# The tail of a one-core transformer block: transposes ahead of most folds, and half of the last norm shared by GpSimd and ScalarE

## The chip, the cores and the metric

The kernel runs as one program on one core of a Trainium2 chip. The time is the device time of one execution in microseconds (us). The kernel before was timed in three runs; the number quoted for it is their median. One further execution was recorded by the hardware profiler, and every duration below comes from that one. Its engines are TensorE (PE, with its weight loads PEld), VectorE (DVE), ScalarE (ACT), GpSimd (POOL) and the queue of SyncE (SP), which issues DMAs.

## The reference, cut to what matters

One layer: a modulated RMSNorm, an input projection into three kinds of heads, an output projection with a gated residual that gives `x1`, then a second modulated RMSNorm and a product-key expert layer (PEER), a second gated residual and a last RMSNorm. The change touches only the end:

```python
# peer: the expert layer's output for 256 tokens x 1024 channels
x = x + g2 * peer                                  # g2: one gate per channel
y = x * rsqrt(mean(x * x, axis=-1) + 1e-6)         # last RMSNorm
out = y * final_norm_g                             # one weight per channel
```

For each of 256 tokens the expert layer picks 16 experts of 16384 in each of 8 heads, and sums `gate * gelu(u_e . h) * v_e` over them.

## The kernel before, in words

All is float32. Tokens are numbered 0 to 255. The expert layer is computed in two ways at once. For the first ND = 160 tokens it is dense: TensorE streams the whole table `peer_u` through `u_chunk` (line 1034) and the whole table `peer_v` through `v_chunk` (line 1090), in 128 chunks each, and the products of gates and activations lie in `A3`. For the other 96 tokens GpSimd gathers the chosen rows by indirect DMAs (line 1917), and VectorE takes their dot products (line 1595) and adds them, weighted, into three tiles `sums[0..2]` (line 1608). Each of these tiles holds 32 tokens, a token's rows spread over four groups of 32 partitions.

The tail begins when the last chunk of `peer_v` has been multiplied. The dense result lies transposed, channels on partitions, in banks 4, 5 and 6 of PSUM, eight blocks `m` of 128 channels by 160 tokens. ScalarE copies banks 4 and 6 (lines 1380 and 1383) and VectorE bank 5 (line 1854) to the SBUF tile `OT`. TensorE then has three kinds of work, in this order:

- six folds (line 1113): a matmul with `fold4` sums the four partition groups of `sums[s]`, for a half (512 channels) of 32 tokens; banks 2 and 3, partitions 32 to 127;
- eight transposes (line 1123) of tokens 0 to 127 of `OT` into banks 0 and 1, four per half; `folded` is counted up once per half;
- eight matmuls (line 1127) that transpose tokens 128 to 159 into banks 2 and 3, partitions 0 to 31, four per half; `folded` again once per half.

So banks 0 to 3 hold the two halves of token block 0 (tokens 0 to 127) and of block 1 (tokens 128 to 255), numbered n = 0 to 3. VectorE runs, for each n, a multiplication of the bank by the gate `g2b` into a scratch place (line 1862; one input in PSUM, one in SBUF) and an addition of that to `x1n` (line 1863; both inputs in SBUF). ScalarE squares each sum with an accumulated row sum (line 1389). Per block VectorE adds the two row sums (`final_sum`, line 1867, two 128x1 inputs in SBUF), ScalarE takes the root (line 1392), VectorE the reciprocal (line 1872), and then VectorE multiplies both halves by the reciprocal and the weights `fin` (line 1874; two SBUF tensors and a per-partition pointer). The order of VectorE's work is written out: residuals 0, 1, 2, `final_sum(0)`, residual 3, `final_norm(0)`, `final_sum(1)`, `final_norm(1)`. SyncE's queue waits for each of the four half blocks in turn and issues its write to HBM (line 690). GpSimd has nothing to do in the tail; its last gather is issued some 30 us before the end of the span. `link` (line 1409) lets VectorE wait for its own instruction. Every engine works its instructions in the order written, and a wait holds up all that stand behind it on that engine. The weights `fin` are loaded into `gate_buf` once the gates are done (line 686).

Of the kernel before, what the change touches and what calls it, by code (L numbers as in the profile page):

```python
# [13 lines left out]
D = 1024  # L14
# [24 lines left out]
SUB = 32  # L39
# [192 lines left out]
LAST_TWO = (4 * SC2 + 2, 4 * SC2 + 3)  # L232

# [99 lines left out]
def build(nc, x_t, ctx_t, cols, rows, sgu_gain, final_gain, constants, sgu_wt, bias_mask, ada_w, w_in,  # L333
# [21 lines left out]
    with ExitStack() as stack:  # L355
# [172 lines left out]
        aside_full = sem("aside_full")  # L528
        own_full = [sem(f"own_full{n}") for n in range(len(OWN))]
# [89 lines left out]
        def _(sp):  # L619
# [67 lines left out]
            for n in range(2 * TB):  # L687
                tb, half = n // 2, slice(n % 2 * 512, n % 2 * 512 + 512)
                sp.wait_ge(out_ready, n + 1)
                sp.dma_start(out[tb * P:(tb + 1) * P, half], x1n[:, tb, half]).then_inc(stored, 16)  # L690
# [4 lines left out]
        def _(pe):  # L695
# [411 lines left out]
            pe.wait_ge(row_used, 2 * DOTS)  # L1107
            pe.wait_ge(a_made, CHUNKS)
            for half in range(2):
                hh = slice(half * 512, half * 512 + 512)  # L1110
                for s in range(SUBS):
                    rows = slice(ND1 + s * SUB, ND1 + (s + 1) * SUB)
                    pe.matmul(bank[2 + half][rows, :], fold4, sums[s][:, hh], start=True, stop=True,
                              tile_position=(0, ND1 + s * SUB))
            for half in range(2):
                for m in range(4 * half, 4 * half + 4):
                    if m == 0:
                        pe.wait_ge(act_out, 1)
                    elif m == 3:
                        pe.wait_ge(dve_out, 1)  # L1120
                    elif m == 6:
                        pe.wait_ge(act_out, 2)
                    mm = pe.transpose(bank[half][:, m % 4 * P:(m % 4 + 1) * P], OT[:, m, 0:P], ident)
                mm.then_inc(folded, 1)
            for half in range(2):
# [23 lines left out]
        def _(act):  # L1149
# [236 lines left out]
            for tb in range(TB):  # L1386
                for n in (2 * tb, 2 * tb + 1):
                    act.wait_ge(res_ready, n + 1)
                    act.activation(A[:, 12288 + n * 512:12288 + n * 512 + 512], x1n[:, tb, n % 2 * 512:n % 2 * 512 + 512], ACT.Square,
                                   accum_out=fsum[:, 0, n:n + 1]).then_inc(fsq_ready, 1)  # L1390
                act.wait_ge(fsum_ready, tb + 1)
                act.activation(fsum[:, 2, tb:tb + 1], fsum[:, 1, tb:tb + 1], ACT.Sqrt, bias=eps[:, :], scale=1.0 / D)\
                   .then_inc(froot_ready, 1)

# [11 lines left out]
        def _(dve):  # L1406
# [450 lines left out]
            def residual(n):  # L1857

                tb, half = n // 2, slice(n % 2 * 512, n % 2 * 512 + 512)
                tmp = A[:, 10240 + n * 512:10240 + n * 512 + 512]  # L1860
                dve.wait_ge(folded, n + 1)
                link(dve.tensor_tensor(tmp, bank[n][:, :], g2b[:, half], ALU.mult))
                dve.tensor_tensor(x1n[:, tb, half], x1n[:, tb, half], tmp, ALU.add).then_inc(res_ready, 1)
# [6 lines left out]
            def final_norm(tb):  # L1870
                dve.wait_ge(froot_ready, tb + 1)
                link(dve.reciprocal(fsum[:, 1, TB + tb:TB + tb + 1], fsum[:, 2, tb:tb + 1]))
                for half in (slice(0, 512), slice(512, D)):
                    dve.scalar_tensor_tensor(x1n[:, tb, half], x1n[:, tb, half], fsum[:, 1, TB + tb:TB + tb + 1],
                                             fin[:, half], ALU.mult, ALU.mult).then_inc(out_ready, 1)

            residual(0)
            residual(1)
            residual(2)
            final_sum(0)  # L1880
            residual(3)
            dve.wait_ge(fin_in, 16)
            dve.wait_ge(res_ready, 2 * TB)
# [6 lines left out]
        def _(pool):  # L1890
# [55 lines left out]
            for n in range(DOTS, 2 * DOTS):  # L1946
                gather(n)

# [75 lines left out]
```

## Time and profile before

| | us |
|---|---|
| median of 3 runs | 890.07 |
| lowest, highest run | 887.4, 891.44 |
| the profiled execution's own time | 888.64 |
| its span in the profile | 886.9 |
| PE busy in the span | 857.2 (97%) |
| DVE busy | 542.9 (61%) |
| ACT busy | 281.1 (32%) |
| POOL busy | 271.2 (31%) |

The span runs from the first to the last recorded event of the execution; its own time is 1.74 us longer, since it also holds what lies around the span. A busy share is an average over stages that have different limits, so for a change to the tail only the rows of the tail tell what it is worth. In the timeline each row gives a start, a duration, engine, line, operation, output <- inputs with their shapes, and in brackets the engine's idle time before it and what ended that. Rows of matmuls merge many instructions; their ends are modelled. The chain of waits is followed back from the last instruction: at each step to what released it.

### The profile page before, as it was taken

How to read it: one execution, taken by the hardware profiler on the slowest of the kernel's cores; microseconds unless marked ns; L12 is line 12 of the kernel's file. 1: busy time of each engine (PE TensorE's matmuls, PEld its weight loads, DVE VectorE, ACT ScalarE, POOL GpSimd, SP SyncE). 2: the span in 40 equal slices, each digit the busy share in tenths (PEclk: the TensorE clock that was granted, in tenths of full speed). 3: DMA queues.
4: the chain of work that ended last, by engine and by line, in shares of the span. 5: the costliest groups of instructions: out<-in, count | busy, mean ns of one | idle time of the engine just before them, and what ended most of it. 6: DMA issues, size and time to landing. Idle time of an engine off the chain costs nothing.

```text
span 886.9 us, 17756 instructions
## 1 busy us (share of the span) xinstructions
PE 857.2 (97%) x6620; PEld 815.3 (92%) x6620; DVE 542.9 (61%) x1073; ACT 281.1 (32%) x684; POOL 271.2 (31%) x245
## 2 busy tenths in 40 slices
PE   3999999999999999999999999999999999999995
PEld 1889996797979999999999999999999999999994
DVE  4567146675899789874547888886333444334447
ACT  4364336856332111122137888860000000000002
POOL 0020002402342343335346433546222223222220
PEclk9999999999999999999999999999999999999998
DMA  9987465042495899999999999999999999999992
GB/s 370 399 325 270 174 231 214 1 191 95 143 331 160 321 409 410 409 399 395 409 409 409 409 396 331 306 356 394 409 409 409 409 409 408 409 409 409 409 409 110
DMA packets 74558, 294.28 MB, mean 332 GB/s; under 512 B 9218, under 2 KB 9346, under 8 KB 67972
## 3 DMA queue, kind: packets, MB, share of 16 engines
q1 hardware_dynamic: 37444, 161.24, 47.0%
q0 software_dynamic: 28416, 100.78, 29.6%
q10 hardware_dynamic: 8640, 31.46, 8.9%
q8 instruction: 40, 0.66, 0.3%
q14 instruction: 18, 0.15, 0.0%
HBM read 290.73 MB, written 1.05 MB: 329 GB/s over the span
## 4 chain that ended last, share of the span: by engine, by line
PE 89%; DMA 4%; DVE 3%; ACT 3%; issue 1%; SPq 0%; ACTq 0%; DVEq 0%; POOL 0%
PE bank L1090 31%; PE bank L1034 29%; PE bank L713 5%; PE bank L714 4%; PE bank L715 4%; PE bank L1043 4%; PE bank L733 2%; DMA stage<-in_peer_u_t 2%; DMA A<-in_ada_w 2%; PE bank L976 1%; PE bank L813 1%; PE bank L752 1%; PE bank L822 1%; PE bank L958 1%; ACT A L1256 1%
## 5 line engine op out<-in xcount | busy, mean ns | idle before, releaser
L1034 PE MATMUL bank<-A,stage 128*128 128x160 f32 x2048 | 286.2, 299 | 0.5 <-DMA stage<-in_peer_u_t 0.2
L1034 PEld LDWEIGHTS bank<-A,stage 128*128 128x128 f32 x2048 | 279.6, 190 | 1.5 <-issue 1.1
L1090 PE MATMUL bank<-A,stage 128*128 128x160 f32 x2048 | 278.3, 299 | 0.0
L1090 PEld LDWEIGHTS bank<-A,stage 128*128 128x128 f32 x2048 | 278.2, 190 | 0.0
L1608 DVE SCALAR_TENSOR_TENSOR sum<-A,row_gate,sum 128x1024 f32<-128x1024 f32 x81 | 104.0, 1284 | 132.8 <-DMA A<-in_peer_v,row_expert 131.5
L1917 POOL DMA_INDIRECT A<-in_peer_v,row_expert x84 | 83.7, 996 | 165.2 <-DVE sum L1608 147.9
L1595 DVE CUSTOM_DVE_ANT_0 A<-A 128x1024 f32<-128x1024 f32 x80 | 97.7, 1222 | 51.7 <-DMA A<-in_peer_u,row_expert 51.5
L1917 POOL DMA_INDIRECT A<-in_peer_u,row_expert x80 | 91.3, 1141 | 122.0 <-DVE row_dot L1595 66.0
L1380 ACT ACTIVATE A<-bank 128x480 f32<-128x480 f32 x1 | 0.6, 572 | 276.3 <-PE bank L1090 276.3
L1312 ACT ACTIVATE A<-bank 128x160 f32 (+1 forms) x88 | 26.7, 303 | 150.3 <-PE bank L1034 150.3
L715 PE MATMUL bank<-h_hi,ring_low 128*128 128x256 f32 x224 | 63.3, 283 | 0.0
L1334 ACT ACTIVATE gate_buf<-gate_buf,choice_t 128x128 f32<-128x128 f32 x160 | 51.1, 390 | 4.4
L1327 ACT ACTIVATE gate_buf<-con,choice_t 128x128 f32<-128x128 f32 x160 | 50.7, 390 | 0.6 <-issue 0.6
L1043 PE MATMUL bank<-gate_buf 128*128 128x128 f32 x320 | 43.7, 280 | 0.9 <-ACT gate_buf L1334 0.9
L1043 PEld LDWEIGHTS bank<-gate_buf 128*128 128x128 f32 x320 | 38.9, 191 | 4.7 <-issue 4.4
L715 PEld LDWEIGHTS bank<-h_hi,ring_low 128*128 128x128 f32 x224 | 42.9, 191 | 0.0
L1401 POOL TENSOR_TENSOR ring_low<-A,lo 128x512 fp32r<-128x512 f32 x4 | 5.0, 1270 | 91.3 <-ACT lo L1218 91.3
L733 PE MATMUL bank<-A,csil 128*32 128x256 f32 x208 | 16.1, 441 | 13.5 <-DMA A<-in_ada_w 13.5
L1917 POOL DMA_INDIRECT last_row<-in_peer_u,row_expert x16 | 20.1, 1259 | 28.8 <-DVE row_dot L1595 20.6
L1810 DVE TENSOR_TENSOR gate_buf<-con,choice_t 128x512 f32<-128x512 f32 x40 | 27.3, 685 | 0.0
L1818 DVE TENSOR_TENSOR A<-A,bank 128x512 f32<-128x512 f32 x40 | 27.1, 679 | 0.0
L1824 DVE TENSOR_TENSOR A<-A,choice 128x160 f32<-128x160 f32 x40 | 13.0, 325 | 22.8 <-ACT choice L1319 22.8
(271 smaller groups left out, 1221.7 us busy)
## 6 DMA issues: line engine op xcount, KB each, us to landing
stage<-in_peer_u_t SPq DMA_DIRECT2D x128, 512.0 KB, 10.0
stage<-in_peer_v SPq DMA_DIRECT2D x68, 512.0 KB, 7.8
stage<-in_peer_v ACTq DMA_DIRECT2D x60, 512.0 KB, 8.4
A<-in_ada_w SPq DMA_DIRECT2D x13, 1024.0 KB, 7.4
A<-in_w_in SPq DMA_DIRECT2D x11, 1024.0 KB, 6.7
stage<-in_ada_w SPq DMA_DIRECT2D x10, 1024.0 KB, 6.9
A<-in_w_q SPq DMA_DIRECT2D x8, 1024.0 KB, 7.4
A<-in_w_out SPq DMA_DIRECT2D x4, 1024.0 KB, 4.8
```

What stands on the lines that cost most here:

```text
L713: pe.matmul(o, a_hi, b_hi, start=(k == 0), stop=False)
L714: pe.matmul(o, a_hi, b_lo, start=False, stop=False)
L715: mm = pe.matmul(o, a_lo, b_hi, start=False, stop=(k == KD - 1))
L733: mm = pe.matmul(o[q, 0:BLK], csil[:, k, :], w[:, k, :], start=(k < 4), stop=(k >= 4), tile_position=(0, 32 * (k % 4)))
L1034: mm = pe.matmul(o, stage[j][:, k * P:(k + 1) * P], H2[:, k, 0:ND], start=(k == 0), stop=(k == KD - 1))
L1043: mm = pe.matmul(bank[4 + j][:, t * NK:(t + 1) * NK], ONE1[:, j, t, :], ONE2[:, j, t, :], start=True, stop=True)
L1090: mm = pe.matmul(bank[b][:, n * ND:(n + 1) * ND], stage[c % SLOTS][:, m * P:(m + 1) * P], A3[:, c, :], start=(c == 0 and n == 0), stop=(c ...
L1327: last = act.activation(ONE2[:, j % 2, t, :], iota, ACT.Square, bias=choice_t[:, 0, bass.ds(g * GT + t, 1)])
L1334: last = act.activation(ONE2[:, j % 2, t, :], ONE2[:, j % 2, t, :], ACT.Relu, bias=choice_t[:, 2, bass.ds(g * GT + t, 1)], scale=-2.0)
L1595: dve.tensor_tensor_reduce(g, g, h2_rows[:, s, :], 1.0, 0.0, ALU.mult, ALU.add, row_dot[:, s, c:c + 1])\
L1608: dve.scalar_tensor_tensor(sums[s][:, :], g, w, sums[s][:, :], ALU.mult, ALU.add)\
L1917: pool.indirect_dma_start(gathered[slot], None, peer_u if n < DOTS else peer_v, bass.IndirectOffsetOnAxis(ap=row_expert[:, s, c:c + 1], ax ...
```

## The change

It has three parts.

1. On TensorE, two folds (the first two tiles, first half) come first, then the eight transposes, then the other four folds (the third tile's first half, all three of the second half), then the matmuls of tokens 128 to 159. The wait for all rows of `sums` moves behind the transposes; ahead of them stands a wait for the rows of the first two tiles alone.
2. The addition of n = 1 goes from VectorE to GpSimd. The multiplications and additions on VectorE are written apart and wait for each other by the semaphore `res_scaled`; VectorE's order is now: scale 0, add 0, scale 1, scale 2, add 2, scale 3, `final_sum(0)`, add 3, `final_norm(0)`, `final_sum(1)`, `final_norm(1)`.
3. Of the last norm, VectorE keeps the first half of each block. For the second half GpSimd multiplies `x1n` by the weights `fin` into a scratch place as soon as that half is summed (`gained`), and ScalarE multiplies this by VectorE's reciprocal (`root_turned`), as a Copy whose scale is a per-partition pointer. ScalarE's order is: squares 0, 1, 2, root of block 0, square 3, second half of block 0, root of block 1, second half of block 1. SyncE's queue waits for the two halves by two semaphores, in the same order of writes as before.

```diff
--- before.py
+++ after.py
@@ -232,6 +232,9 @@
 LAST_TWO = (4 * SC2 + 2, 4 * SC2 + 3)
 
 
+POOL_ADDS = 1
+
+
 def row_slot(n):
 
     return n % GATHER if n < EARLY else (n - EARLY) % WIDE_GATHER
@@ -526,6 +529,8 @@
             sem, ("consts_in", "x_in", "ctx_in", "cols_in", "gating_in", "bias_in", "subkeys_in", "g2_row_in"))
         own_split = sem("own_split")
         aside_full = sem("aside_full")
+        res_scaled, res_added, gained, root_turned, act_out_ready = map(
+            sem, ("res_scaled", "res_added", "gained", "root_turned", "act_out_ready"))
         own_full = [sem(f"own_full{n}") for n in range(len(OWN))]
         ring_full = [[sem(f"ring{r}_full{s}") for s in range((RING, RING, SIDE)[r])] for r in range(3)]
         bank_full = [sem(f"bank_full{b}") for b in range(8)]
@@ -686,7 +691,10 @@
             sp.dma_start(fin, final_gain).then_inc(fin_in, 16)
             for n in range(2 * TB):
                 tb, half = n // 2, slice(n % 2 * 512, n % 2 * 512 + 512)
-                sp.wait_ge(out_ready, n + 1)
+                if n % 2:
+                    sp.wait_ge(act_out_ready, n // 2 + 1)
+                else:
+                    sp.wait_ge(out_ready, n // 2 + 1)
                 sp.dma_start(out[tb * P:(tb + 1) * P, half], x1n[:, tb, half]).then_inc(stored, 16)
             sp.wait_ge(stored, 16 * 2 * TB)
 
@@ -1104,14 +1112,16 @@
                 v_chunk(c)
 
 
-            pe.wait_ge(row_used, 2 * DOTS)
+            def fold(s, half):
+
+                rows, hh = slice(ND1 + s * SUB, ND1 + (s + 1) * SUB), slice(half * 512, half * 512 + 512)
+                pe.matmul(bank[2 + half][rows, :], fold4, sums[s][:, hh], start=True, stop=True,
+                          tile_position=(0, ND1 + s * SUB))
+
             pe.wait_ge(a_made, CHUNKS)
-            for half in range(2):
-                hh = slice(half * 512, half * 512 + 512)
-                for s in range(SUBS):
-                    rows = slice(ND1 + s * SUB, ND1 + (s + 1) * SUB)
-                    pe.matmul(bank[2 + half][rows, :], fold4, sums[s][:, hh], start=True, stop=True,
-                              tile_position=(0, ND1 + s * SUB))
+            pe.wait_ge(row_used, 2 * DOTS - ROWS)
+            for s in range(SUBS - 1):
+                fold(s, 0)
             for half in range(2):
                 for m in range(4 * half, 4 * half + 4):
                     if m == 0:
@@ -1122,6 +1132,10 @@
                         pe.wait_ge(act_out, 2)
                     mm = pe.transpose(bank[half][:, m % 4 * P:(m % 4 + 1) * P], OT[:, m, 0:P], ident)
                 mm.then_inc(folded, 1)
+            pe.wait_ge(row_used, 2 * DOTS)
+            fold(SUBS - 1, 0)
+            for s in range(SUBS):
+                fold(s, 1)
             for half in range(2):
                 for m in range(4 * half, 4 * half + 4):
                     mm = pe.matmul(bank[2 + half][0:ND1, m % 4 * P:(m % 4 + 1) * P], OT[:, m, P:ND], ident,
@@ -1383,14 +1397,38 @@
             act.activation(OT[:, 6:8, :].rearrange("p m t -> p (m t)"), bank[6][:, 0:2 * ND], ACT.Copy)\
                .then_inc(act_out, 1)
             act.activation(fsum[:, 2, TB:TB + 1], eps[:, :], ACT.Sqrt)
-            for tb in range(TB):
-                for n in (2 * tb, 2 * tb + 1):
-                    act.wait_ge(res_ready, n + 1)
-                    act.activation(A[:, 12288 + n * 512:12288 + n * 512 + 512], x1n[:, tb, n % 2 * 512:n % 2 * 512 + 512], ACT.Square,
-                                   accum_out=fsum[:, 0, n:n + 1]).then_inc(fsq_ready, 1)
+            def squared(n):
+
+                if n == POOL_ADDS:
+                    act.wait_ge(res_added, 1)
+                else:
+                    act.wait_ge(res_ready, n + 1 - (n > POOL_ADDS))
+                tb, half = n // 2, slice(n % 2 * 512, n % 2 * 512 + 512)
+                act.activation(A[:, 12288 + n * 512:12288 + n * 512 + 512], x1n[:, tb, half], ACT.Square,
+                               accum_out=fsum[:, 0, n:n + 1]).then_inc(fsq_ready, 1)
+
+            def final_root(tb):
+
                 act.wait_ge(fsum_ready, tb + 1)
                 act.activation(fsum[:, 2, tb:tb + 1], fsum[:, 1, tb:tb + 1], ACT.Sqrt, bias=eps[:, :], scale=1.0 / D)\
                    .then_inc(froot_ready, 1)
+
+            def scaled_out(tb):
+
+                act.wait_ge(gained, tb + 1)
+                act.wait_ge(root_turned, tb + 1)
+                at = 10240 + (2 * tb + 1) * 512
+                act.activation(x1n[:, tb, 512:D], A[:, at:at + 512], ACT.Copy,
+                               scale=fsum[:, 1, TB + tb:TB + tb + 1]).then_inc(act_out_ready, 1)
+
+            squared(0)
+            squared(1)
+            squared(2)
+            final_root(0)
+            squared(3)
+            scaled_out(0)
+            final_root(1)
+            scaled_out(1)
 
 
         def quarter_rest(eng, n):
@@ -1854,13 +1892,20 @@
             dve.tensor_copy(OT[:, 3:6, :].rearrange("p m t -> p (m t)"), bank[5][:, 0:3 * ND]).then_inc(dve_out, 1)
 
 
-            def residual(n):
+            def scaled_at(n):
+                return A[:, 10240 + n * 512:10240 + n * 512 + 512]
+
+            def scale_residual(n):
+
+                half = slice(n % 2 * 512, n % 2 * 512 + 512)
+                dve.wait_ge(folded, n + 1)
+                dve.tensor_tensor(scaled_at(n), bank[n][:, :], g2b[:, half], ALU.mult).then_inc(res_scaled, 1)
+
+            def add_residual(n):
 
                 tb, half = n // 2, slice(n % 2 * 512, n % 2 * 512 + 512)
-                tmp = A[:, 10240 + n * 512:10240 + n * 512 + 512]
-                dve.wait_ge(folded, n + 1)
-                link(dve.tensor_tensor(tmp, bank[n][:, :], g2b[:, half], ALU.mult))
-                dve.tensor_tensor(x1n[:, tb, half], x1n[:, tb, half], tmp, ALU.add).then_inc(res_ready, 1)
+                dve.wait_ge(res_scaled, n + 1)
+                dve.tensor_tensor(x1n[:, tb, half], x1n[:, tb, half], scaled_at(n), ALU.add).then_inc(res_ready, 1)
 
             def final_sum(tb):
                 dve.wait_ge(fsq_ready, 2 * tb + 2)
@@ -1869,18 +1914,20 @@
 
             def final_norm(tb):
                 dve.wait_ge(froot_ready, tb + 1)
-                link(dve.reciprocal(fsum[:, 1, TB + tb:TB + tb + 1], fsum[:, 2, tb:tb + 1]))
-                for half in (slice(0, 512), slice(512, D)):
-                    dve.scalar_tensor_tensor(x1n[:, tb, half], x1n[:, tb, half], fsum[:, 1, TB + tb:TB + tb + 1],
-                                             fin[:, half], ALU.mult, ALU.mult).then_inc(out_ready, 1)
-
-            residual(0)
-            residual(1)
-            residual(2)
+                dve.reciprocal(fsum[:, 1, TB + tb:TB + tb + 1], fsum[:, 2, tb:tb + 1]).then_inc(root_turned, 1)
+                dve.wait_ge(root_turned, tb + 1)
+                dve.scalar_tensor_tensor(x1n[:, tb, 0:512], x1n[:, tb, 0:512], fsum[:, 1, TB + tb:TB + tb + 1],
+                                         fin[:, 0:512], ALU.mult, ALU.mult).then_inc(out_ready, 1)
+
+            scale_residual(0)
+            add_residual(0)
+            scale_residual(POOL_ADDS)
+            scale_residual(2)
+            add_residual(2)
+            scale_residual(3)
             final_sum(0)
-            residual(3)
+            add_residual(3)
             dve.wait_ge(fin_in, 16)
-            dve.wait_ge(res_ready, 2 * TB)
             final_norm(0)
             final_sum(1)
             final_norm(1)
@@ -1945,6 +1992,18 @@
                         .then_inc(gate_in, 16)
             for n in range(DOTS, 2 * DOTS):
                 gather(n)
+            pool.wait_ge(res_scaled, POOL_ADDS + 1)
+            tb, half = POOL_ADDS // 2, slice(POOL_ADDS % 2 * 512, POOL_ADDS % 2 * 512 + 512)
+            at = 10240 + POOL_ADDS * 512
+            pool.tensor_tensor(x1n[:, tb, half], x1n[:, tb, half], A[:, at:at + 512], ALU.add).then_inc(res_added, 1)
+            pool.wait_ge(fin_in, 16)
+            for tb in range(TB):
+                if tb == 0:
+                    pool.wait_ge(res_added, 1)
+                else:
+                    pool.wait_ge(res_ready, 2 * TB - 1)
+                at = 10240 + (2 * tb + 1) * 512
+                pool.tensor_tensor(A[:, at:at + 512], x1n[:, tb, 512:D], fin[:, 512:D], ALU.mult).then_inc(gained, 1)
 
 
 def bias_places():
```

## Rows read from the trace of the kernel before

**Rows 1.** The page, part 4: the chain that ended last, by engine

```profile
PE 89%; DMA 4%; DVE 3%; ACT 3%; issue 1%; SPq 0%; ACTq 0%; DVEq 0%; POOL 0%
```

**Rows 2.** The chain, from 860 us on: start, us, what

```profile
874.53 0.60 PE bank L1123 x4
882.43 0.30 ACT fsum L1392
882.96 0.75 DVE x1n L1874
```

**Rows 3.** Timeline, 872 to 876 us: start, us, engine, line, operation

```profile
872.45 0.65 DVE L1854 COPY A<-bank 128x480 f32<-128x480 f32 x1
872.62 1.92 PE L1113 MATMUL bank<-sum,con 128*32 128x512 f32 x12
872.72 0.44 ACT L1383 ACTIVATE A<-bank 128x320 f32<-128x320 f32 x1 [0.79 <-PE bank L1090]
874.47 1.09 PE L1123 MATMUL bank<-con,A 128*128 128x128 f32 x8
875.16 0.69 DVE L1862 TENSOR_TENSOR A<-bank,g2b 128x512 f32<-128x512 f32 x1 [2.06 <-PE bank L1123]
875.49 1.94 PE L1127 MATMUL bank<-con,A 128*32 128x128 f32 x16
```

**Rows 4.** Timeline, 877 to 881 us, DVE and ACT, same columns

```profile
877.82 0.68 DVE L1862 TENSOR_TENSOR A<-bank,g2b 128x512 f32<-128x512 f32 x1
878.54 0.69 DVE L1863 TENSOR_TENSOR x1n<-x1n,A 128x512 f32<-128x512 f32 x1
879.15 0.15 DVE L1867 TENSOR_TENSOR fsum<-fsum 128x1 f32<-128x1 f32 x1
879.53 0.61 ACT L1389 ACTIVATE A<-x1n 128x512 f32<-128x512 f32 x1
880.05 0.19 ACT L1389 ACTIVATION_READ_ACCUMULATOR A<-x1n 128x1 f32 x1
```

**Rows 5.** GpSimd: line 1401 (ns min/median/max), then two from the timeline

```profile
L1401 POOL TENSOR_TENSOR ring_low<-A,out_hi x8: 1261/1276/1297, 157.0 to 170.9; 128x512 fp32r<-128x512 f32 x8
195.97 0.63 ACT L1271 ACTIVATE A<-A 128x512 f32<-128x512 f32 x1
196.68 0.74 POOL L1902 TENSOR_TENSOR A<-A 128x256 f32<-128x256 f32 x1 [24.53 <-ACT A L1271]
```

**Rows 6.** Timelines of GpSimd and of VectorE; last, line 1507 (ns)

```profile
50.99 3.77 POOL L1896 TENSOR_TENSOR A<-A 128x1024 f32<-128x1024 f32 x2 [50.54 <-ACT A L1226]
50.99 6.52 POOL L1896 TENSOR_TENSOR A<-A 128x1024 f32<-128x1024 f32 x3 [50.54 <-ACT A L1226]
53.52 3.40 DVE L1507 TENSOR_TENSOR ring_low<-A,lo 128x2048 fp32r<-128x2048 f32 x1 [2.73 <-ACT lo L1204]
252.07 4.80 POOL L1906 TENSOR_TENSOR ring_low<-A,query_hi 128x2048 fp32r<-128x2048 f32 x1 [7.38 <-ACT query_hi L1204]
253.78 3.14 DVE L1584 SCALAR_TENSOR_TENSOR A<-choice 128x32 uint32<-128x32 f32 x1
L1507 DVE TENSOR_TENSOR ring_low<-A,query_hi x3: 2284/2285/2293, 192.4 to 213.9; 128x2048 fp32r<-128x2048 f32 x3
```

**Rows 7.** ScalarE lines 1281 and 1223 (ns); a root in the timeline

```profile
L1281 ACT ACTIVATE A<-A,mod x8: 492/493/508, 205.5 to 210.2; 128x256 f32<-128x256 f32 x8
L1223 ACT ACTIVATE h_hi<-A x8: 399/410/419, 151.7 to 190.1; 128x256 fp32r<-128x256 f32 x8
178.25 0.69 ACT L1145 ACTIVATE gate_buf<-bank,eps 128x512 f32<-128x512 f32 x1
```

**Rows 8.** Last two writes' issues; stretches, last columns DMA share and GB/s

```profile
883.73 0.99 SPq L690 DMA_DIRECT2D out_x<-x1n  x2
884.40:884.60 0.20, 0.00 (x0) 0.00 (x0) 0.00 (x0) 0.00 (x0) 0.00 (x0) 0.50 0.19 72
885.80:886.00 0.20, 0.00 (x0) 0.00 (x0) 0.00 (x0) 0.00 (x0) 0.00 (x0) 0.50 0.75 277
```

## Prediction

> **What bounds the kernel now.** The page's chain by engine comes first: TensorE carries 89% of it, VectorE and ScalarE 3% each, and GpSimd nothing [rows 1]. The reader sees from it that a change behind TensorE's last chunk can only touch a few per mille. The body, up to 872.6 us of a span of 886.9, is left as it is by the diff; what is priced here is the 14.3 us behind it. The chain of that stretch [rows 2] and its timeline [rows 3, 4] show three steps. TensorE runs six folds, then transposes; only when four transposes are done, at 875.16, can VectorE start (it had been free since 873.10). From there VectorE alternates multiplication and addition without a pause and sets the pace. At the end comes a short relay for block 1, root, reciprocal, product: the root starts at 882.43, the product at 882.96, and its first half ends at 883.71 [rows 2].
>
> **What sets the end.** The last two writes are issued from 883.73, the second as soon as its half is ready, 0.66 us later (0.99 us for two issues of 0.33) [rows 8]. DMA traffic starts within 884.40 to 884.60 (share 0.19, so at about 884.56) and ends within 885.80 to 886.00 (share 0.75, so at about 885.95): 1.4 us for two writes of 256 KB, 0.7 each, back to back [rows 8]. The first write's issue therefore sets the end. If the second half comes earlier its write only queues behind the first. So I measure everything by one moment: the end of VectorE's product for the first half of block 1, now 883.71. That ScalarE finishes the other half at the same time, not 0.7 us later, is worth nothing.
>
> **TensorE.** Six folds took from 872.62 to 874.47, 0.31 each; the eight transposes 1.02; the first product on VectorE started 0.69 after the first transpose [rows 3]. With two folds ahead the transposes start at 872.62 + 0.62 = 873.24, and scale 0 at 873.93, not 875.16. The copies that the transposes wait for, at 873.10 (VectorE) and 873.16 (ScalarE) [rows 3], are just in time, the first being asked for by the fourth transpose at about 873.6. But the work ahead of the last eight matmuls is the same six folds and eight transposes, so they start at 875.49 as before and take 1.94 [rows 3]: bank 2 is full at about 876.50, bank 3 at 877.43. Of the 1.23 us won for n = 0 and 1, what is late next is bank 2.
>
> **VectorE up to there.** Multiplication to addition is 0.72 from start to start, addition to the next 0.61 [rows 4]. Scale 0 873.93, add 0 874.65, scale 1 875.26 to 875.94. Scale 2 waits 0.6 us for bank 2, 876.50 in place of 877.82 [rows 4]; add 2 is ready at 877.22. Taking add 1 away saves VectorE 0.6 us, but that falls into this wait. So far we are 1.32 us ahead.
>
> **GpSimd's three instructions.** Its TENSOR_TENSOR of 128x512 took 1.28 (1.26 to 1.30), and it starts 0.08 after what it waited for (196.60 to 196.68) [rows 5]. The addition for n = 1 runs 876.02 to 877.30. The question is what GpSimd costs VectorE. Two places show it. At 53.52 VectorE's line 1507, two SBUF inputs, met GpSimd: GpSimd's second addition ended at 54.76, VectorE at 56.92, after 3.40 in place of 2.29, and GpSimd's third ended at 57.51 [rows 6]. VectorE's end is 2.16 after GpSimd's, its own duration less 0.13; GpSimd's third, 0.74 when alone [rows 5], ended 0.59 after VectorE. At 253.78 an instruction over only 32 columns took 3.14, until 256.92, just as GpSimd's 4.80 ended at 256.87 [rows 6]. I read: VectorE instructions with two SBUF inputs and GpSimd's TENSOR_TENSOR exclude each other, and the one that waited ends 0.13 to 0.15 short of a full duration after the other. The multiplications read a bank and one SBUF tile; I take them as free. The additions, both final sums and the products with `fin` have two SBUF inputs.
> The Trainium skill, "SBUF — State Buffer", in the section on who interferes with whom, states an exclusive lock for the whole instruction. The trace agrees with the exclusion but shows the head start of 0.13 to 0.15; taking the rule to its letter, with full durations behind each release, the moment would come at 883.52 and the time be 889.9.
>
> **The sum.** Add 2, waiting since 877.22, ends at 877.91. GpSimd's product for block 0 is ready at 877.35, waits for add 2, and ends at 877.91 + 1.13 = 879.04. A square takes 0.71 from start to the end of its accumulator [rows 4]: square 1 from 877.35 to 878.06, square 2 to 878.77. `final_sum(0)`, a 128x1 addition of 0.15 [rows 4], could run at 878.44 but has two SBUF inputs: it waits for GpSimd and ends at 879.09. Behind it on VectorE stands add 3: 879.01 to 879.70. Root 0 ends at 879.42, hidden. From root to product are 0.23 us for the reciprocal and its waits (882.73 to 882.96) [rows 2]; here the product 0 is ready at 879.85, GpSimd's product for block 1 at 879.78, and either may win. If GpSimd does, it ends at 881.06, VectorE at 881.68, `final_sum(1)` at 881.75; if VectorE does, GpSimd ends at 881.73 and `final_sum(1)` at 881.78. The two agree. Square 3 is done at 880.45 and hidden. Root 1 0.33 later, product from 882.34, first half finished at 883.09. **The gain is 883.71 - 883.09 = 0.6 us.**
>
> **ScalarE.** Its scaled Copy of 128x512 I price at 0.61 [rows 4] plus 0.08 for the pointer, the difference of 493 and 410 ns between lines 1281 and 1223 [rows 7]: 0.7. The first runs 880.45 to 881.15, ahead of root 1, which can't start before 881.78: hidden by GpSimd's hold on VectorE; without that cover it is on the path (rival 1). The second runs beside VectorE's last product, and its write queues behind. Copies of line 1223 follow the root of 178.25 [rows 7] with no table load among ScalarE's rows until the Gelus, so I expect none here. If one were needed for each change between Copy and Sqrt, two loads would stand ahead of root 1.
> SyncE's split waits, VectorE's extra semaphore waits and TensorE's moved wait cost nothing: the same waits were there as `link`, and all gathered rows are summed before VectorE's copy of 872.45 [rows 3], which stands behind them.
>
> **Rivals.**
> 1. *No exclusion worth the name*: GpSimd's instructions interfere little. `final_sum(0)` ends at 878.59, add 3 at 879.20, product 0 starts at 879.33; square 3 ends at 879.95, then the Copy of 0.7 stands ahead of root 1, which ends at 880.96; product 1 ends at 881.94. Gain 1.8, time 888.3. Against it stand both places of [rows 6]; for it only that neither has TensorE and ScalarE in this tail. Chance 0.15.
> 2. *GpSimd keeps its turn* (slower): its product for block 0 goes ahead of add 2. Then add 2 ends at 877.35 + 1.28 + 0.56 = 879.19, add 3 at 880.48, GpSimd's product 1 at 881.84, VectorE's product 0 at 882.46, `final_sum(1)` at 882.53, and the moment is 883.84: 0.13 later than before, time 890.2. It decides as soon as add 2 is ready over 0.13 us later than 877.22, that is if bank 2 fills after 876.63. For it: my 876.50 is a modelled end. Against: in [rows 6] VectorE, waiting first, went ahead of GpSimd's next. Chance 0.3.
> The Trainium skill, "SBUF — State Buffer", the same section, has a rule for this one: issue order decides who blocks. GpSimd's product needs nothing but its own addition; if it counts as issued behind it at once, the rule gives rival 2, and no row here separates the two.
> 3. *The parts cancel otherwise*: TensorE's order brings less than shown, since the copies come late by more than 0.5 us, and the time stays at 890.1. Both copies end at least 0.4 us ahead of their need. Chance 0.05.
> The forecast has 0.5.
>
> **How the numbers follow.** The profiled execution's own time is 888.64, 1.43 below the median of 890.07; its forecast is 888.0, and that of the median 890.07 - 0.6 = 889.5. The three runs lie between 887.4 and 891.44, which is more than any case here moves. The range takes in rival 1 at 888.3 and rival 2 at 890.2 and about 1 us of that scatter on each side: 887.3 to 891.2. A measurement of this kernel tells about 0.5%, 4.5 us, from no change: faster would need under 885.6, slower over 894.5. The largest gain is 1.8, the largest loss 0.13, so only scatter or something unseen in the body leads there: 0.04 and 0.03, and 0.93 for within.
>
> **What would show it.** In the profile after, counted from the end of line 1090's last matmul: VectorE's first multiplication 1.2 us after it, not 2.5; an idle VectorE before scale 2, ended by TensorE; `final_sum(0)` of line 1867 lasting over 0.5 us, not 0.15; the first or second GpSimd product longer than 1.28; no table load behind the last root; two output issues back to back, with 1.4 us of traffic. A `final_sum` of 0.15 everywhere means rival 1. An addition for n = 2 of over 1.5 us means rival 2. The forecast is wrong if the moment comes over 1 us from 0.6 us ahead of before, or if the stretch ahead of the tail differs.

## The result, and the profile after

The changed kernel takes 892.92 us (median of 20 runs, 889.82 to 894.29); the kernel before takes 889.07 in 20 runs (887.25 to 892.56). The ratio is 1.0031, with a 95% interval of 1.0021 to 1.0041: slower by 2.8 us. The means, 892.34 and 889.53, lie 2.8 us apart, the medians 3.85. The profiled execution's own time is 891.03 and its span 888.9, 2.0 more than before.

The timeline of the changed kernel's tail answers to [rows 3] and [rows 4]; columns are start, us, engine, line, operation, and idle time before with its releaser.

```profile
872.03 1.05 PE L1118 MATMUL bank<-sum,con 128*32 128x512 f32 x4
872.13 0.44 ACT L1397 ACTIVATE A<-bank 128x320 f32<-128x320 f32 x1 [0.79 <-PE bank L1098]
...
873.01 1.09 PE L1133 MATMUL bank<-con,A 128*128 128x128 f32 x8
873.70 0.69 DVE L1902 TENSOR_TENSOR A<-bank,g2b 128x512 f32<-128x512 f32 x1 [1.21 <-PE bank L1133]
...
875.81 1.26 POOL L1998 TENSOR_TENSOR x1n<-x1n,A 128x512 f32<-128x512 f32 x1 [19.04 <-DVE A L1902]
876.04 0.69 DVE L1902 TENSOR_TENSOR A<-bank,g2b 128x512 f32<-128x512 f32 x1 [0.32 <-PE bank L1141]
876.77 0.85 DVE L1908 TENSOR_TENSOR x1n<-x1n,A 128x512 f32<-128x512 f32 x1
...
877.21 1.54 POOL L2006 TENSOR_TENSOR A<-x1n,gate_buf 128x512 f32<-128x512 f32 x1
...
878.14 0.62 DVE L1912 TENSOR_TENSOR fsum<-fsum 128x1 f32<-128x1 f32 x1
...
878.69 0.68 DVE L1908 TENSOR_TENSOR x1n<-x1n,A 128x512 f32<-128x512 f32 x1
...
879.45 1.27 POOL L2006 TENSOR_TENSOR A<-x1n,gate_buf 128x512 f32<-128x512 f32 x1 [0.70 <-DVE x1n L1908]
879.47 1.79 DVE L1919 SCALAR_TENSOR_TENSOR x1n<-x1n,fsum,gate_buf 128x512 f32<-128x512 f32 x1
...
880.03 0.71 ACT L1421 ACTIVATE x1n<-A,fsum 128x512 f32<-128x512 f32 x1
...
881.36 0.29 ACT L1413 ACTIVATE fsum<-fsum,eps 128x1 f32<-128x1 f32 x1 [0.63 <-DVE fsum L1912]
...
881.89 0.75 DVE L1919 SCALAR_TENSOR_TENSOR x1n<-x1n,fsum,gate_buf 128x512 f32<-128x512 f32 x1
881.95 0.72 ACT L1421 ACTIVATE x1n<-A,fsum 128x512 f32<-128x512 f32 x1 [0.29 <-DVE fsum L1917]
```

To compare profiles I count from the start of ScalarE's copy of bank 6, which begins as the last matmul of the chunks ends: 872.72 before [rows 3], 872.13 here. VectorE and ScalarE are ahead of the kernel before all the way. VectorE's first multiplication starts at +1.57 (before +2.44), and the moment of the forecast, the end of VectorE's product for the first half of block 1, comes at +10.51 (before +10.99). GpSimd's and VectorE's two-input instructions shut each other out, as the trace of the kernel before had let one expect: `final_sum(0)` of 128x1 lasts 0.62 us, VectorE's product of block 0 1.79, GpSimd's product 1.54. ScalarE is done at 882.67. Yet the span ends at 888.9, 6.2 us later. SyncE's queue had issued its last write by 883.50 (the last three issues in one row):

```profile
881.68 1.82 SPq L698 DMA_DIRECT2D out_x<-x1n  x3
```

The instructions at the end of the program, which count as no engine's busy time, show the rest. In this view (one source line; duration in ns min/median/max, first and last start in us) the changed kernel has:

```profile
L358 POOLq DRAIN  x1: 9235/9235/9235, 879.4 to 879.4; - x1
...
L358 SPq DRAIN  x1: 7/7/7, 885.6 to 885.6; - x1
L358 SPq EVENT_SEMAPHORE  x1: 17/17/17, 888.8 to 888.8; - x1
```

The same view of the kernel before:

```profile
L355 POOLq DRAIN  x1: 18257/18257/18257, 856.3 to 856.3; - x1
...
L355 SPq DRAIN  x1: 7/7/7, 886.6 to 886.6; - x1
L355 SPq EVENT_SEMAPHORE  x1: 17/17/17, 886.8 to 886.8; - x1
```

Each engine closes with a DRAIN, an instruction that stands behind all its others; SyncE's comes behind its wait for the last write. In all 13 profiles of this document the span ends 0.2 us behind the later of two of them, SyncE's and GpSimd's. The row of a DRAIN can start while the instruction ahead of it still runs, so what counts is its end. Before, GpSimd's drain stood behind its last gather (856.48 to 857.42) and was over at 874.5, hidden by the whole tail; the end followed SyncE's drain of 886.6 by 0.2 us. Now GpSimd works until 880.71, and its drain ends at 888.64: 7.93 us behind its last instruction, and 3.1 us after SyncE's drain of 885.6. The tail, from the start of ScalarE's copy to the end of the span, is 16.74 us and was 14.13: 2.61 longer, where SyncE's drain alone would have made it 0.49 shorter.

The span doesn't hold all of the time. What lies around it (own time less span, mean over all timed runs, each span known to 0.1 us) is 1.79 to 1.80 us in the kernel before and 2.15 in the changed one. This 0.35 us comes on top of the 2.61; why it is there was not tried.

### The profile page after: what moved, and what is told of

Same layout as the page of the kernel before. It is cut to its first block, busy times and chain, and to the rows that moved or that the text cites. A ratio compares the mean times of both kernels' runs of the same rounds, so it can differ in the third digit from the quotient of the medians.

```text
span 888.9 us, 17761 instructions
## 1 busy us (share of the span) xinstructions
PE 854.4 (96%) x6620; PEld 812.9 (91%) x6620; DVE 542.4 (61%) x1070; ACT 282.6 (32%) x686; POOL 276.8 (31%) x248
## 4 chain that ended last, share of the span: by engine, by line
PE 85%; DMA 6%; ACT 3%; DVE 2%; issue 1%; POOL 1%; SPq 0%; ACTq 0%; DVEq 0%
PE bank L1098 31%; PE bank L1042 27%; PE bank L721 4%; PE bank L1051 4%; PE bank L722 4%; PE bank L723 4%; DMA stage<-in_peer_u_t 4%; PE bank L741 2%; DMA A<-in_ada_w 2%; PE bank L760 1%; PE bank L821 1%; PE bank L830 1%; PE bank L984 1%; PE bank L966 1%; DMA A<-in_w_q 1%
## 5 line engine op out<-in xcount | busy, mean ns | idle before, releaser
L1964 POOL DMA_INDIRECT A<-in_peer_u,row_expert x80 | 94.3, 1178 | 119.9 <-DVE row_dot L1633 76.6
```

What stands on the lines that cost most here:

```text
L1964: pool.indirect_dma_start(gathered[slot], None, peer_u if n < DOTS else peer_v, bass.IndirectOffsetOnAxis(ap=row_expert[:, s, c:c + 1], ax ...
```

## The experiments

Theory D: GpSimd's closing drain, some 8 us behind its last instruction whatever that is, ends the program. Rival P: the products on GpSimd cost VectorE the time. Rival T: the drain is long only behind a TENSOR_TENSOR. Rival G: the drain ends the program, but it is long only because of the gathers, and a drain taken earlier makes it short. The table gives every profile in us, counted from the start of ScalarE's copy of bank 6 (last GpSimd instruction's end, closing drain's end, SyncE's drain, end of the span), and the measured ratio to the kernel before, timed beside it, with its 95% interval. Where a kernel has a second drain, the third column is that of the closing one. order_sum_ahead and best are each measured twice.

| kernel | last GpSimd | its drain | SyncE's drain | end | ratio (interval) |
|---|---|---|---|---|---|
| before | -15.31 | 1.79 | 13.91 | 14.13 | 1 |
| changed | 8.58 | 16.51 | 13.42 | 16.74 | 1.0031 (1.0021 to 1.0041) |
| late_memset | 8.29 | 16.23 | 14.12 | 16.46 | 1.0026 (1.0012 to 1.0040) |
| no_last_product | 6.63 | 14.56 | 12.70 | 14.79 | 1.0009 (0.9993 to 1.0025) |
| add_alone | 4.93 | 12.87 | 12.89 | 13.11 | 0.9983 (0.9970 to 0.9997) |
| mid_drain | 15.10 | 23.01 | 19.94 | 23.25 | one run, 898.66 us |
| after_early_drain | 9.27 | 9.34 | 14.12 | 14.34 | 0.9993 (0.9980 to 1.0005) |
| after_early_drain_2 | 8.58 | 8.65 | 13.42 | 13.64 | 1.0000 (0.9985 to 1.0014) |
| order_alone | -15.35 | 1.80 | 13.04 | 13.26 | 0.9994 (0.9981 to 1.0008) |
| order_sum_ahead | -14.06 | 2.26 | 12.60 | 12.82 | 0.9982 (0.9971 to 0.9993) |
| order_sum_ahead_2 | -13.27 | 2.59 | 12.65 | 12.87 | 0.9986 (0.9974 to 0.9999) |
| best | 4.93 | 5.00 | 12.46 | 12.68 | 0.9993 (0.9982 to 1.0005) |
| best_2 | 4.93 | 5.01 | 12.46 | 12.68 | 0.9987 (0.9972 to 1.0001) |

**One idle instruction on GpSimd, late.**

```diff
--- kernel before
+            pool.wait_ge(res_ready, 2 * TB)
+            pool.memset(spare[:, :], 0.0).then_inc(late, 1)
```

The tile `spare` (128x1) and the semaphore `late` are declared besides.

> The kernel before, plus one GpSimd memset of 128x1 into a tile nobody reads, waiting for the last residual. Tail = span end less the start of ScalarE's copy of bank 6: 14.2 us before, 16.8 in the changed kernel. Theory D (GpSimd's closing drain takes about 8 us after its last instruction, whatever that is, and the program ends behind it): the memset runs about 8.0 us into the tail, the drain ends 8 us later, tail 16.3 to 16.5, time +2.2 us. Rival P (the changed kernel lost its time to products on GpSimd that hold up VectorE): tail 14.2, no change. Rival T (the drain is long only behind a TENSOR_TENSOR): tail 14.2, drain under 2 us behind the memset.

GpSimd's timeline and the closing instructions of this kernel:

```profile
881.57 0.10 POOL L1951 MEMSET spare<- 128x1 f32 x1 [22.79 <-DVE x1n L1865]
```

```profile
L355 POOLq DRAIN  x1: 8050/8050/8050, 881.5 to 881.5; - x1
...
L355 SPq DRAIN  x1: 7/7/7, 887.5 to 887.5; - x1
L355 SPq EVENT_SEMAPHORE  x1: 17/17/17, 889.8 to 889.8; - x1
```

A memset of 0.10 us, whose result nobody reads, ends at 881.67; the drain ends at 881.5 + 8.05, 7.94 behind it by the table, 2.1 after SyncE's. The time rises by 0.26%, the end in the table by 2.33 us, which is 0.26% of 889. No part of the change is in this kernel. Rival T falls, and rival P isn't needed for the loss. Theory D and rival G both fit so far.

**The same change with GpSimd's drain taken earlier.**

```diff
--- changed kernel
             for n in range(DOTS, 2 * DOTS):
                 gather(n)
+            pool.drain()
             pool.wait_ge(res_scaled, POOL_ADDS + 1)
```

> The changed kernel with one drain more on GpSimd, behind its last gather and ahead of its first work in the tail, where GpSimd idles for 19 us. Theory D (about 8 us fixed behind any last instruction): the closing drain stays at about 8 us and the tail at 16.8. Rival G (the closing drain is long since it settles the gathers' descriptors, once): the early drain takes that over, unseen, the closing one ends by the time of SyncE's last wait, tail 13.7 to 13.9, 3 us faster than the changed kernel.

> The changed kernel with the drain on GpSimd ahead of the tail, once more, since in the first profile VectorE's rows came 1.4 us late. With rows on time (VectorE's copy of bank 5 within 0.3 us of ScalarE's of bank 6) the tail should be 13.6 to 13.7; then sharing the halves costs 0.5 to 0.6 us against the addition alone (13.1), by GpSimd's products holding up final_sum(0) and VectorE's product of block 0. Time -0.5 against before.

The second run's GpSimd row, the added drain (line 1995), and the closing instructions:

```profile
881.98 1.27 POOL L2007 TENSOR_TENSOR A<-x1n,gate_buf 128x512 f32<-128x512 f32 x1 [0.70 <-DVE x1n L1908]
```

```profile
L1995 POOLq DRAIN  x1: 17201/17201/17201, 859.8 to 859.8; - x1
```

```profile
L358 POOLq DRAIN  x1: 1375/1375/1375, 881.9 to 881.9; - x1
...
L358 SPq DRAIN  x1: 7/7/7, 888.1 to 888.1; - x1
L358 SPq EVENT_SEMAPHORE  x1: 17/17/17, 888.2 to 888.2; - x1
```

The added drain takes 17.20 us from 859.8 to 877.0, while GpSimd waits anyway for VectorE's first results. The closing drain now starts with the product of 881.98 and lasts 1.38: it ends 0.07 us behind that product. The end of the span is SyncE's again. The tail is 13.64, 3.1 shorter than in the changed kernel, with every other instruction of the change in its place; the ratios 0.9993 and 1.0000 have intervals that don't touch that of the changed kernel. So the drain is the loss. Theory D in its first form (8 us behind any last instruction, tail 16.8) missed here, and rival G forecast it. That it is the gathers since the last drain, and not GpSimd's other work or the time since then, is the likely reading but not shown: no kernel here has a long stretch without gathers behind a drain. Against the kernel before this tail is 0.49 us shorter, but the measured time doesn't show it: both intervals hold 1, and what lies around the span is 2.04 to 2.06 us, 0.25 more than there. In the first of the two runs VectorE's copy of bank 5 came at +1.19, with the rows late, and that execution's tail is 0.70 longer.

**Half the gathers behind the last drain.**

```diff
--- changed kernel
+            pool.drain()
             for n in range(DOTS, 2 * DOTS):
                 gather(n)
```

> The changed kernel with a drain on GpSimd half way, between the 96 gathers of the first table (with the loads of row_gate) and the 96 of the second, and none ahead of the tail. The closing drain now stands behind half of GpSimd's DMAs. If its length is their number (so much per DMA not yet settled), it ends about 4.0 to 4.5 us behind GpSimd's last product, tail 13.7 to 13.9. If it is a fixed price for any gather since the last drain, it stays at 7.9, tail 16.7. The body may be longer, since the drain holds the second gathers up; only the tail is read.

```profile
887.23 1.27 POOL L2007 TENSOR_TENSOR A<-x1n,gate_buf 128x512 f32<-128x512 f32 x1 [2.51 <-DVE x1n L1908]
```

```profile
L358 POOLq DRAIN  x1: 9219/9219/9219, 887.2 to 887.2; - x1
```

GpSimd's last product ends at 888.50 and the drain at 887.2 + 9.22 = 896.4, 7.91 behind. Half the gathers, the same price: it isn't so much per gather. The forecast tail of 16.7 was missed, for another reason. The added drain lasted until 585.5, 9.9 us behind the last DMA that GpSimd had issued (of line 1990), so the second table's first gather was issued at 586.28, against 574.70 in the changed kernel. The rows came late, VectorE's copy of bank 5 started at +5.32, and the tail is 23.25. Only the closing drain's length is read from this kernel. What GpSimd does in those 7.9 us these profiles don't show.

**GpSimd's work cut step by step.** First without its last product:

```diff
--- changed kernel
+SHARED = (0,)
...
-            for tb in range(TB):
+            for tb in SHARED:
                 ...
                 pool.tensor_tensor(A[:, at:at + 512], x1n[:, tb, 512:D], fin[:, 512:D], ALU.mult).then_inc(gained, 1)
```

VectorE makes both halves of block 1, and ScalarE only the second half of block 0. The waits of VectorE, ScalarE and SyncE follow; VectorE waits for all four sums ahead of its first product.

> The changed kernel, but VectorE makes both halves of block 1's last product; GpSimd ends with its product for block 0. Drain theory: GpSimd's last instruction ends 6.5 to 6.7 us into the tail, its drain 7.95 later at 14.5, tail 14.7 to 14.8, that is +0.6 against the kernel before and -2.0 against the changed one. If the drain weren't what ends the program, the tail would be VectorE's, 13.3 to 13.6.

```profile
878.63 1.53 POOL L2014 TENSOR_TENSOR A<-x1n,gate_buf 128x512 f32<-128x512 f32 x1
```

```profile
L359 POOLq DRAIN  x1: 9495/9495/9495, 878.6 to 878.6; - x1
```

The drain ends 7.93 behind the product of 880.16, 1.9 after SyncE's. Then without both products; the addition for n = 1 is all that GpSimd keeps:

```diff
--- changed kernel
+SHARED = ()
...
-            for tb in range(TB):
+            for tb in SHARED:
```

> The changed kernel without its third part: GpSimd makes only the addition for n = 1 and VectorE both halves of both blocks' last product. Theory D: GpSimd's last instruction ends about 5.0 us into the tail, its drain at 13.0, hidden behind the writes; the tail is VectorE's, 12.9 to 13.3, time -1.0 to -1.3 against before. Rival P (only contention matters): the same tail here, so this run tells D from P only together with the memset. Theory X (any GpSimd work in the tail costs some 3 us at the end): tail 15 or more.

The addition ends at +4.93 and the drain at +12.87, a hair ahead of SyncE's at +12.89: just hidden. Theory X of the expectation (15 us or more with any GpSimd work in the tail) falls: the end is +13.11, 1.02 less than before, and the ratio of 0.9983 (to 0.9997) is faster than before. The same GpSimd is on the path or off it by when its last instruction ends. Four kernels with an undrained queue of gathers (8.58, 8.29, 6.63 and 4.93) give 7.93, 7.94, 7.93 and 7.94.

**Part 1 alone.** The kernel before with TensorE's new order and nothing else:

```diff
--- kernel before
-            pe.wait_ge(row_used, 2 * DOTS)
             pe.wait_ge(a_made, CHUNKS)
-            for half in range(2):
-                ...
+            pe.wait_ge(row_used, 2 * DOTS - ROWS)
+            for s in range(SUBS - 1):
+                fold(s, 0)
             for half in range(2):
                 ...
+            pe.wait_ge(row_used, 2 * DOTS)
+            fold(SUBS - 1, 0)
+            for s in range(SUBS):
+                fold(s, 1)
```

`fold` is the function of the changed kernel.

> The kernel before with part 1 alone: TensorE's transposes ahead of four folds. No GpSimd in the tail. All theories: VectorE starts 1.2 us earlier and, taking 1.33 us for each multiplication and addition, reaches scale 2 at about the moment bank 2 fills, so it keeps all of it: tail 13.0 in place of 14.2, time -1.2 us. If bank 2 bounds instead, scale 2 waits and the tail is 13.1 to 13.5.

The end comes 0.87 earlier, not 1.2: VectorE starts at +1.57, not +2.44, and keeps all of it, since scale 2 starts at +4.23 without a wait. The tail of 13.26 lies in the range that the expectation gives for a wait for bank 2, but there was none: the smaller start explains it. The ratio, 0.9994 (0.9981 to 1.0008), can't tell 0.87 us (0.9990) from none; the profile can.

**Two versions meant to beat both kernels.** To part 1 alone:

```diff
--- order_alone
-                for half in (slice(0, 512), slice(512, D)):
+                for h in range(2):
+                    half = slice(h * 512, h * 512 + 512)
                     ...
+                    if tb == 0 and h == 0:
+                        final_sum(1)
             final_norm(0)
-            final_sum(1)
             final_norm(1)
```

> The kernel with part 1 alone, and final_sum(1) put between VectorE's two products of block 0, so that ScalarE's root for block 1 runs beside the second. No GpSimd in the tail. VectorE's first product of block 1 starts 0.4 us earlier: tail 12.8 to 12.9 in place of 13.26, time -1.3 against before. If the first write of block 1 is held up behind the second of block 0 on the DMA queues, the tail stays within 0.2 of 13.26.

> The same kernel as order_sum_ahead, once more beside best: tail 12.8, time -1.3 us against before (ratio 0.9985), within 0.2 us of best.

And with GpSimd's addition and the early drain besides:

```diff
--- add_alone
                 gather(n)
+            pool.drain()
             pool.wait_ge(res_scaled, POOL_ADDS + 1)
...
+                if tb == 0:
+                    final_sum(1)
                 if tb not in SHARED:
                     ...
             final_norm(0)
-            final_sum(1)
             final_norm(1)
```

> Part 1, GpSimd's addition for n = 1 (no product on GpSimd or ScalarE), a drain on GpSimd behind its last gather, and final_sum(1) between the two products of block 0. Drain theory: the closing drain is over 1.4 us after GpSimd's start of that addition's drain, far ahead of SyncE's; tail 12.6 to 12.7, time -1.4 against before. Against order_sum_ahead the addition on GpSimd is worth 0.1 to 0.2, since VectorE waits for bank 2. If the early drain delays the last gathers' rows, VectorE's copy of bank 5 comes over 1 us late and nothing is gained.

> The same kernel as best, once more beside order_sum_ahead: tail 12.7, time -1.4 us against before (ratio 0.9984). If the early drain costs something in the body, the tail is 12.7 again but the ratio is nearer to 1 than that of order_sum_ahead_2.

`order_sum_ahead` ends at +12.82 and +12.87 and is faster than the kernel before in both measurements, 0.9982 and 0.9986, with both intervals below 1. Its first write of block 1 wasn't held up, which would have left the tail within 0.2 of 13.26. The version with the addition on GpSimd ends 0.14 to 0.19 earlier in its profiles, as expected, but measures 0.9993 and 0.9987 with intervals that reach 1. The intervals of the two overlap, so a difference in the measured time isn't shown. But what lies around the span can account for the missing lead: it is 1.96 to 1.97 us in `best` and 1.80 to 1.81 in `order_sum_ahead` (1.79 in `add_alone`, which has GpSimd's addition but no early drain). The version to take is `order_sum_ahead`, which puts no new work on GpSimd or ScalarE.

## Why the prediction was wrong

I forecast 889.5 from 890.07, 0.6 us faster, with a range of 887.3 to 891.2. Measured are 892.92 and, by the ratio, 2.8 us slower. Point by point:

- **What sets the end: the step that failed.** "The first write's issue therefore sets the end. ... So I measure everything by one moment." This moment came 0.48 us earlier than before, and the time rose. The end has two conditions, SyncE's wait for its writes and the other engines' closing drains, of which GpSimd's is the late one. The first is as I had it: SyncE's drain ended 2.92 us behind the moment before and 2.91 after. In the trace of before the second was met 12.1 us ahead of SyncE's (1.79 against 13.91) and appears in neither the chain nor the busy times. What GpSimd does behind its last instruction was put at nothing, and what hid it was not named: GpSimd had finished early, and the change took that away. "GpSimd, nothing" in the chain said only that its drain was hidden. With the step mended by the measured 7.93 behind the last product, which I had at 881.06 on the scale of before, the drain ends at 888.99 and the span at 889.2 in place of 886.9, 2.3 us slower. Measured are 2.61 in the tail, since the last product ended 8.58 us into it and not 8.34, and 0.35 more around the span.
- **TensorE's order.** Right in kind, too large in size. I spread 1.85 us evenly over six folds, 0.31 each. But the folds of a half use three different groups of columns and run at once (the rows of the last section): three folds take the time of one, and so do two. Two folds took 0.98 (872.03 to 873.01), six 1.85. VectorE's start was 0.87 us earlier, not 1.23. Most of this error of 0.36 us fell into VectorE's wait for bank 2, which was 0.32 long and not 0.6: scale 2 started 3.91 us into the tail, 0.13 later than the forecast of 3.78.
- **GpSimd's three instructions.** The addition took 1.26 (forecast 1.28), and the first product, waiting, ended 1.13 after add 2 (877.62 to 878.75), as priced. Add 2 itself ended 0.55 after GpSimd's addition, not beside it: 0.85 long in place of 0.69, 0.16 us that I had taken for none. `final_sum(0)` ended 0.01 after GpSimd's product. Of the race for block 1, GpSimd won (879.45 against 879.47), and VectorE's product ended at 881.26, 0.54 after GpSimd's end. That the other order would cost the same no run shows.
- **The rule on the pair of SBUF ports** (the Trainium skill, "SBUF — State Buffer", section "Who interferes with whom"). It states an exclusive lock for the whole instruction. These rows show the exclusion once more, but not full durations behind each release: VectorE's product of 0.75 ended 0.54 after GpSimd's, GpSimd's of 1.27 ended 1.13 after add 2. Rival 2's reading of issue order did not come about: add 2, which had been waiting, went ahead of GpSimd's queued product in the changed kernel and in both after_early_drain profiles.
- **ScalarE.** Its scaled Copy took 0.71 (forecast 0.70), with no table load behind it.
- **The sum of the tail without the drain.** after_early_drain_2 has the changed kernel's tail with the drain out of the way, row by row on VectorE: 13.64 against 14.13, 0.49 us shorter; the forecast was 0.6. So apart from the drain the sum came out to 0.1 us, in part by luck: the error of 0.36 in TensorE's order fell into a wait.
- **The rivals.** None contained the mechanism, and the largest loss that I allowed for was 0.13 us. The slower rival, GpSimd going ahead of add 2, was worth just that, a twentieth of the loss. No `final_sum(0)` of 0.15 (it lasted 0.62) and no add 2 of over 1.5 us (0.85): by their own signs rivals 1 and 2 both fell. Rival 3 fell with VectorE's earlier start.

## What to carry to other kernels

When work is put on an engine that had finished early, look at what that engine still has to do behind its last instruction: in this kernel GpSimd's closing drain needed 7.9 us after gathers, so its last instruction had to end 8 us ahead of SyncE's drain, or the drain had to be taken beforehand, where the engine waits anyway. The chain and the busy times leave such instructions out; the view of the line that holds the closing instructions (355 before, 358 after) shows them. And sharing work between VectorE and GpSimd lengthened VectorE's instructions with two SBUF inputs that met GpSimd's (0.15 to 0.62 us, 0.75 to 1.79). A plain reordering of the same work on VectorE (0.87 us by TensorE's order, 0.4 more by one moved `final_sum`) was worth more than three engines sharing it.

## What the runs showed of the hardware that was not expected

- GpSimd's closing drain ended 7.91 to 7.94 us behind its last instruction in five kernels, whatever that was (a memset of 0.10 us or a product of 1.27) and though its last gather had been issued over 18 us before that. After 96 gathers it was the same as after 192. With a drain between gathers and last instruction it ended 0.07 us behind it. A drain right behind the last gather took longer, 14.9 to 17.2 us from that gather's end in eight profiles. In all eight it ended 4.4 us behind the last packet of GpSimd's DMA queue (4.38 to 4.43; in the kernel before the last packet ended at 870.12 and the drain at 874.51), so most of it is the wait for the gathered data. The 4.4 us don't hold for every drain: that of mid_drain at line 1993, behind the loads of `row_gate`, ended 8.9 us behind the queue's last packet.
- Matmuls of 32 columns in different groups of TensorE's array run at once. In the kernel before the six folds (two passes each) come in four groups of three matmuls, at 872.62, 873.07, 873.50 and 873.93, though each matmul lasts 0.59 or more. Their weight loads run up to one group ahead:

```profile
872.62 0.15 PEld L1113 LDWEIGHTS bank<-sum,con 128*32 128x32 f32 x6 [0.17 <-DVE sum L1608]
...
873.07 0.12 PEld L1113 LDWEIGHTS bank<-sum,con 128*32 128x32 f32 x3 [0.31 <-issue]
...
873.50 0.12 PEld L1113 LDWEIGHTS bank<-sum,con 128*32 128x32 f32 x3 [0.31 <-issue]
```

  The changed kernel's two folds need two passes too, at 872.03 and 872.48, before the transposes of 873.01. Behind the transposes the folds and the matmuls of tokens 128 to 159 (line 1141), written one after the other in the program, appear interleaved:

```profile
874.49 0.60 PE L1118 MATMUL bank<-sum,con 128*32 128x512 f32 x3
...
874.52 0.60 PE L1141 MATMUL bank<-con,A 128*32 128x128 f32 x4
...
874.92 0.59 PE L1118 MATMUL bank<-sum,con 128*32 128x512 f32 x1
...
874.96 0.60 PE L1141 MATMUL bank<-con,A 128*32 128x128 f32 x4
...
875.35 0.59 PE L1118 MATMUL bank<-sum,con 128*32 128x512 f32 x1
875.39 0.60 PE L1141 MATMUL bank<-con,A 128*32 128x128 f32 x4
```

  So the last matmul ended 3.86 us into the tail (875.99), and 4.71 (877.43) before, where the transposes stood between the two kinds. VectorE's scale 2 started at 876.04, right behind the last fold (875.35 + 0.59 = 875.94), although by its modelled end bank 2 was written at 875.12. This fits a count of `folded` that goes up in program order, behind all folds; it was not tried by itself.
